# MLA attention units scheduled over five turns instead of seven in a four-layer transformer kernel

## The reference, cut to what matters

```python
def hybrid_layer(x, ...):
    h = x @ w_in
    o_sb = stick_breaking_attention(...)
    o_mla = mla_mixer(mla_cols, ...)      # 4 heads, 64 + 32 wide, softmax over the past
    o_rwkv = rwkv7_mixer(rwkv_cols, ...)  # 8 heads, a recurrence over 512 tokens
    mix = concatenate([o_sb, o_mla, o_rwkv]) @ w_o
    x = layer_norm(DEEPNORM_ALPHA * x + mix, ...)
    ...                                   # gated feed-forward, second layer norm

def causal_softmax_attention(q, k, v, scale):   # inside mla_mixer, by blocks of 128 queries
    s = (q @ k.T) * scale                  # past keys only, the rest is -max
    p = softmax(s)
    return p @ v
```

## Time and profile before

| | |
|---|---|
| median of 3 runs | 2958.18 us (2952.99, 2958.18, 2962.57) |
| profiled execution, its own time | 2945.16 us |
| its span | 2943.2 us |
| PE / DVE / ACT / POOL busy | 95% / 49% / 34% / 6% |
| mean granted clock of PE | 0.965 |
| turns of layer 1, turn 7 to the end | about 1512.6 to 1701 us |
| turns of layer 2, turn 7 to the end | about 2333.9 to 2513 us |

### The profile page before, as it was taken

How to read it: one execution, slowest core, us unless ns; L and a number is a source line. 1 busy time by engine, 2 the same in 40 slices (tenths; PEclk the granted TensorE clock), 3 DMA queues, 4 the chain that set the end, 5 groups by cost and what they waited for, 6 DMA issues and landing times.

```text
span 2943.2 us, 45217 instructions
## 1 busy us (share of the span) xinstructions
PE 2802.0 (95%) x20028; PEld 2308.4 (78%) x20028; DVE 1446.1 (49%) x2266; ACT 988.8 (34%) x1490; POOL 169.9 (6%) x166
## 2 busy tenths in 40 slices
PE   8999999999999999999989799999999897899998
PEld 7877888878777888887758778888787587788887
DVE  4575433444465443433454584443634545743436
ACT  4343422232334333223352233232334432242422
POOL 0200000001100000000003300000000023100000
PEclk9998999999979999999979899999999998999999
DMA  5102222223003322221000123222121001132221
GB/s 195 45 1 96 86 100 98 89 74 113 15 1 114 113 87 99 100 92 55 17 1 3 46 99 129 100 86 100 63 86 43 1 3 46 72 118 105 92 101 58
DMA packets 31011, 216.83 MB, mean 74 GB/s; under 512 B 3680, under 2 KB 3936, under 8 KB 6368
## 3 DMA queue, kind: packets, MB, share of 16 engines
q1 hardware_dynamic: 30816, 213.94, 20.3%
HBM read 211.83 MB, written 2.10 MB: 73 GB/s over the span
## 4 chain that ended last, share of the span: by engine, by line
PE 88%; DVE 8%; ACT 2%; issue 1%; PEld 0%; PEldq 0%; DMA 0%; ACTq 0%; SPq 0%; DVEq 0%
PE PS L570 81%; PE PS L573 3%; PE PS L771 2%; DVE SC L1383 1%; DVE R L1383 1%; DVE SM L1394 1%; DVE X L1391 1%; PE PS L854 1%; PE PS L1187 1%; PE PS L1137 1%; DVE SM L1383 1%; DVE LN L1383 0%; PE PS L764 0%; ACT LN L2173 0%; PEld PS L570 0%
## 5 line engine op out<-in xcount | busy, mean ns | idle before, releaser
L570 PE MATMUL PS<-H,SPL 128*128 128x512 f32 (+1 forms) x4560 | 1054.4, 391 | 5.4 <-DVE H L1391 3.9
L570 PEld LDWEIGHTS PS<-H,SPL 128*128 128x128 f32 (+1 forms) x4560 | 851.6, 188 | 188.4 <-issue 6.8
L1383 DVE TENSOR_TENSOR SPL<-RAW,SPL 128x2048 fp32r<-128x2048 f32 (+3 forms) x192 | 429.6, 2239 | 679.1 <-ACT SPL L2173 675.8
L2173 ACT ACTIVATE SPL<-RAW 128x2048 fp32r<-128x2048 f32 (+3 forms) x192 | 358.0, 1868 | 781.3 <-PE PS L570 754.9
L570 PE MATMUL PS<-SPL,Uu 128*128 128x512 f32 x2592 | 589.8, 389 | 0.0
L570 PEld LDWEIGHTS PS<-SPL,Uu 128*128 128x128 f32 x2592 | 486.5, 188 | 101.0
L570 PE MATMUL PS<-SPL,H 128*128 128x512 f32 (+2 forms) x2016 | 432.1, 375 | 2.4 <-DVE SPL L1383 1.6
L570 PEld LDWEIGHTS PS<-SPL,H 128*128 128x128 f32 x2016 | 363.8, 189 | 69.0 <-DVE SPL L1383 2.1
L2173 ACT ACTIVATE R<-PS 128x512 f32<-128x512 f32 (+1 forms) x154 | 88.5, 584 | 184.3 <-PE PS L570 154.6
L1383 DVE TENSOR_TENSOR R<-R,PS 128x512 f32<-128x512 f32 (+1 forms) x98 | 64.7, 661 | 107.4 <-PE PS L570 92.0
L2173 ACT ACTIVATE Uu<-R 128x512 fp32r<-128x512 f32 x108 | 68.3, 632 | 142.1 <-DVE R L1383 142.1
(11 more groups left out here) (239 smaller groups left out, 2503.5 us busy)
## 6 DMA issues: line engine op xcount, KB each, us to landing
RAW<-in_wA SPq DMA_DIRECT2D x84, 1024.0 KB, 4.8
RAW<-in_wB SPq DMA_DIRECT2D x84, 1024.0 KB, 4.8
RAW<-in_wAo SPq DMA_DIRECT2D x8, 1024.0 KB, 4.9
RAW<-in_wBo SPq DMA_DIRECT2D x8, 1024.0 KB, 5.1
LN<-in_ln SPq DMA_DIRECT2D x4, 1024.0 KB, 5.8
P<-in_pB SPq DMA_DIRECT2D x2, 1920.0 KB, 8.4
RAW<-in_wBm SPq DMA_DIRECT2D x4, 704.0 KB, 4.0
X<-in_x SPq DMA_DIRECT2D x4, 512.0 KB, 5.7
```

The lines of the kernel that those rows point to most:

```text
L570: return pe.matmul(out, l_, r_, start=start, stop=stop)
L1383: return v.tensor_tensor(out, a, b, o)
L2173: return a.activation(out, in_, f, scale=scale)
```

## The change

A unit without a sink and without a forget gate (so an MLA unit) is `short`: DVE negates the maxima in the turn in which it finds them, ACT's exponentials come one turn after the scores instead of three, and PE's transpositions two turns after the scores instead of four. A unit takes five turns. POOL's count goes from 28 to 20. No instruction is added or removed.

```diff
         class Unit(namedtuple("Unit", "nh per k0 k1 score val dst sink fq fb n")):
+            @property
+            def short(self):
+                return self.fq is None and self.sink is None
...
@@ tensor: attend
                 ins.then_inc(s.at_s[i], 1)
                 yield
                 yield
-                yield
-                yield
+                if not u.short:
+                    yield
+                    yield
                 pe.wait_ge(s.at_e[i], n(("at_e", i)))
...
@@ vector: attend
                     own(red(mx, u.scores(i), ALU.max))
+                if u.short:
+                    ts(ms, mx, -1.0, None, ALU.mult, None).then_inc(s.at_n[i], 1)
                 yield
...
-                else:
-                    ts(ms, mx, -1.0, None, ALU.mult, None).then_inc(s.at_n[i], 1)
-                yield
-                yield
+                if not u.short:
+                    yield
+                    yield
                 v.wait_ge(s.at_e[i], n(("at_e", i)))
...
@@ gpsimd: strand
-                yield from idle(28, ("at", i))
+                yield from idle(20, ("at", i))
```

## The result

The changed kernel takes 2966.78 us (median of 7 runs, 2961.54 to 2970.2), the kernel before 2952.99 us beside it (7 runs, 2948.78 to 2962.57). The ratio is 1.005, with a 95% interval of 1.0035 to 1.0065: **slower by about 14 us**, where 7 us faster were forecast, and outside the range.

The account below looks back on a forecast made before the run. PE bounds the kernel, with time to win where it idles or runs at its lower clock. Stretches -9.6 and -5.8, clock +2 x 3.3, units 2 x (-0.5 + 1.3): -7.2 us, from 2958.2 to 2951.0 us; range 2940 to 2962.

Parts of the forecast that it names:

- The stretch behind turn 27: Turn 27 to turn 36: 46.0 us with moved work, against 55.6 and 51.8 before; 9.6 and 5.8 us less.
- the clock: One fall of PE's clock per layer, likeliest at the 4.1 us wait with turn 35's level behind it: 3.3 us.
- The three waits: PE waits in turns 31, 32 and 34 because queues are in order: 2.4, 2.6 and 4.1 us.
- The second rival: The post zone stays what it was: both clock falls in every layer, -0.6 us, 2957.6 us; chance 0.18.
- the earlier load: Earlier load of the output weights, with POOL's idle turns: 0, at a DMA share of 0.16 to 0.19.
- Turns 27 to 30: Turns behind the start of prep(2) without post: PE work 11.0 us and waits 4.4, together 15.3 us.
- Turns 31 to 35: Turns with both posts among the levels: 17.8 us of PE work and 9.1 of waiting, 26.9 us.
- The units themselves: Reordered steps of the four units: -0.5 for the second and +1.3 for the third, per layer; others 0.
- I take 0: First unit, turns 8 and 9: exponentials ahead of copies, offset by work moved into idle time; ends -1.5 and +2.
- Turns 11 to 13: Second unit, priced as turns 12 to 14: +0.7 us idle, -1.2 for scores off half clock, together -0.5.
- Turn 19: Third unit, turns 18 and 19: reductions, negations and exponentials come before turn 18's copies; +1.3 us, ends 0 and 2.
- The slower rival, the first unit on the wrong side of the queues: Turns 8 to 10: turn 11 comes late, 9.2 us a layer, +11.2 us in all, 2969.4 us; chance 0.08.

Follow-up runs that it names:

- the spread run: Changed kernel with post(1) four turns later, squares of post(0) and post(1) one turn later, output-weight loads held; ratio 0.9923 to the kernel before.
- the units were measured alone: Changed kernel with its flags set eight turns later, so prep(2), prep(3) and the posts begin in turn 35 as before; ratio 1.0036 to the kernel before.
- with the flags held, units of six turns: Changed kernel with six-turn units, exponentials and all behind them one turn later, prep(2), prep(3) and posts from turn 35 as before; ratio 0.9972 to the kernel before.

## Why the prediction was wrong

**What bounds the kernel.** Right: time is won or lost where PE stands still or runs at the lower clock inside these turns, and the hole behind turn 35 was real. `pairs` gave 6.7 and 4.6 us as soon as the posts were gone from it.

**The stretch behind turn 27.** Forecast 42.2 us plus 3.3 for the clock; measured 56.4 and 54.6. The order of the work was read rightly, and so was PE's work: 28.8 us of products, against 29.83 in the spread run at a clock of 0.95. The three waits were nearly right in sum: 2.4, 2.6 and 4.1 against 2.64, 1.60 and 5.76. The term that failed is **the clock**. The step said "the likeliest place for a fall is that one" and took one fall of 3.3 us per layer. PE was busy 38.64 us for those products, 8.8 more than the 29.83, at 0.79; in layer 2 36.96 us, 7.1 more. There was not one fall but one behind nearly each wait of 1.6 us and more: behind the piece of 2.63 us, the waits of 2.21 and 2.64 us, the 1.60 (layer 1 alone) and the 5.76. Behind 1.28 and 0.47 us the products ran at full clock, and the wait of 1.19 us fell into a low stretch that had already begun. The second rival had both falls per layer, 6.6 us, and even that was too little. The other part is idle time: 17.8 us against 13.5, of which 2.6 is the piece without a releaser. The prediction set the earlier load "0", with a DMA share of 0.16 to 0.19 as the reason. The share was the wrong thing to look at: what counted was that PE, which was full, stood still for 2.6 us while the loads ran.

The miss is also not where the prediction looked for danger alone. Turns 27 to 30, which hold no `post`, were put at 15.3 us and take 22.3 and 22.6 (idle 7.8 and 7.5 for 4.4, busy 14.5 and 15.0 for 11.0). Turns 31 to 35, with both `post`s, were put at 26.9 and 3.3 for the clock and take 34.2 and 32.0.

The rule of the Trainium skill (TensorE: Matmul & The Clock Gate, section Terms), throttled time x (1 - K/N), was set aside in the prediction since most low time lay under DVE's. Behind the change it lay under PE's. An estimate by that page's rule for the stretch from turn 27 to turn 36: a clock of 0.79 over 56.4 us against 0.95 over 35.1 makes 11.8 - 1.8 = 10.1 us of lost clock. The rows show 8.8 more busy, so the rule overstates here by 1.3 us, where my 3.3 understated by 5.5.

**The units themselves.** Forecast +0.8 us a layer. Turn 27 of the changed kernel ends 7.9 and 6.9 us later after turn 7; less the 3.8 us of work that moved there, **+4.1 and +3.1**, and 6.7 where the units were measured alone. Turn 8 first. ACT's rows of layer 1:

```profile
1532.95 0.69 ACT L2176 ACTIVATE RAW<-PS,SM 128x512 f32<-128x512 f32 x1 [5.25 <-DVE SM L1393]
...
1535.62 1.09 ACT L2180 ACTIVATE HA<-PS 128x512 f32<-128x512 f32 x2
```

ACT waited 5.25 us for the maxima before it began its four exponentials, and the copies that PE waits for came behind them: 4.09 us of idle PE, 5.73 in layer 2. That was foreseen, and it was made up for by the idle time that went elsewhere: turns 7 to 10 have 6.0 us of idle time before and 4.9 now. The step "I take 0" for the first unit holds. What failed are the later ones. Turns 11 to 13 were put at 0.7 us more idle time (and -1.2 for the clock) and have 1.7 and 1.3 us more. Turn 19 was forecast at +1.3 and measured +2.1. And turns 25 to 27 were not priced at all: they have 2.1 us of idle time in layer 1 (0.96 for ACT, 1.10 without a releaser), 1.7 more than before, and in layer 2 no more than before. Added up for layer 1, 1.7 + 2.1 + 1.7 - 1.1 is 4.4 us, against the 4.1 found; in layer 2, 1.3 + 2.0 - 0.6 is 2.7, against 3.1.

The slower rival, the first unit on the wrong side of the queues, was therefore not what happened, though the sign was its own.

**The sum.** Behind turn 27 (with the moved work) +4.6 and +6.6 us where -6.3 and -2.5 were forecast; in front +4.1 and +3.1 for +0.8 each; behind turn 36 +3.6 and 0.0. In layer 1 that last part has a piece of 1.60 us without a releaser, right behind the third load.

**The sign.** What would make the prediction wrong had been named: 50 us or more at a clock of 0.7. It was 56 us at 0.79 (54.6 at 0.81 in layer 2). Its chance, 0.18, came with a price of no gain at all, when the falls behind its waits were enough for a loss.

## What to carry to other kernels

Before a chain is moved next to another, look at every in-order queue that both use, the short operations too: the price was one square of 0.63 us that waited for DVE ahead of two copies, and one turn of distance for it was worth 8 to 9 us a layer. Shorter is no aim of its own: with the flags held, units of six turns beat those of five clearly and those of seven by 0.28%, by where their steps land. And price the products behind each wait of some 3 us of a busy PE at the low clock, not behind one of several: here it was so behind 12 of 13 such waits.
